# Eighteen differences and eighteen products of a chunked recurrence moved from GpSimd to VectorE, and two score copies from VectorE to ScalarE

## The reference, cut to what matters

```python
G = jnp.cumsum(gc, axis=2)
o_inter = jnp.einsum('bhtk,bhkv->bhtv', qc * jnp.exp(G), state)
diff = G[:, :, :, None, :] - G[:, :, None, :, :]
decay = jnp.exp(jnp.where(causal[:, :, None], diff, -jnp.inf))
scores = jnp.einsum('bhtsk,bhsk->bhts', qc[:, :, :, None, :] * decay, kc)
o_intra = jnp.einsum('bhts,bhsv->bhtv', scores, vc)
```

## Time and profile before

| | |
|---|---|
| median of 3 runs | 3371.41 us (3369.54 to 3372.2) |
| the profiled execution's own time | 3371.84 us |
| its span | 3370.0 us, so 1.84 us lie around it |
| PE busy over the span | 3061.2 us, 91% |
| DVE, ACT, POOL busy | 1454.9, 827.7, 849.2 us |
| the stage with the two mixers | about 430 to 767 us of the span |

### The profile page before, as it was taken

The page is one execution under the profiler, slowest core; times in us unless marked ns, Lnnn a source line. Parts: engine busy times, 40 slices in busy tenths (PEclk is TensorE's granted clock), DMA queues, the critical chain, the costliest instruction groups (busy, mean ns, idle before and its releaser), DMA issues.

```text
span 3370.0 us, 36149 instructions
## 1 busy us (share of the span) xinstructions
PE 3061.2 (91%) x15301; PEld 2521.8 (75%) x15301; DVE 1454.9 (43%) x2167; ACT 827.7 (25%) x1087; POOL 849.2 (25%) x555
## 2 busy tenths in 40 slices
PE   8889946569999999999999989799999999999997
PEld 7768735457788888887977889766667878787785
DVE  4766447754433333335325244311125443334335
ACT  3211232221211111221237222211111322222221
POOL 0332324441312111223311255300212111111113
PEclk9989966669999999999999999899999999999998
DMA  4112120112211111110311200211030111111111
GB/s 136 57 54 76 42 76 26 51 56 94 75 38 50 50 51 50 38 50 26 104 32 38 61 16 20 69 50 38 25 113 26 50 42 46 50 50 38 50 50 75
DMA packets 152513, 180.47 MB, mean 54 GB/s; under 512 B 6352, under 2 KB 127888, under 8 KB 152352
## 3 DMA queue, kind: packets, MB, share of 16 engines
q1 hardware_dynamic: 143680, 166.51, 15.9%
q10 hardware_dynamic: 8672, 11.65, 1.0%
HBM read 158.05 MB, written 20.09 MB: 53 GB/s over the span
## 4 chain that ended last, share of the span: by engine, by line
PE 76%; DVE 12%; POOL 4%; ACT 3%; issue 3%; DMA 2%; SPq 0%; ACTq 0%; DVEq 0%; POOLq 0%
PE bank L127 75%; DVE f L158 5%; POOL f L158 4%; DVE f L166 2%; PE bank L142 2%; DVE f L175 1%; ACT f L147 1%; DVE f L163 1%; DVE r L158 1%; DVE f L184 1%; ACT r L150 1%; DMA f<-gr_s 1%; ACT f L150 1%; DMA f<-x 0%; DMA f<-w_in 0%
## 5 line engine op out<-in xcount | busy, mean ns | idle before, releaser
L127 PE MATMUL bank<-r,r 128*128 128x512 f32 (+4 forms) x11592 | 2450.4, 372 | 48.3 <-DVE r L158 25.3
L127 PEld LDWEIGHTS bank<-r,r 128*128 128x128 f32 x11592 | 2018.9, 190 | 470.6 <-issue 52.1
L158 POOL TENSOR_TENSOR f<-f 128x512 f32<-128x512 f32 (+5 forms) x313 | 409.6, 1316 | 1770.6 <-ACT f L147 611.7
L158 DVE TENSOR_TENSOR f<-f,bank 128x512 f32<-128x512 f32 (+2 forms) x519 | 318.4, 635 | 453.4 <-PE bank L127 451.9
L127 PE MATMUL bank<-f 128*128 128x128 f32 (+7 forms) x2328 | 343.8, 317 | 115.8 <-DVE f L158 54.7
L158 DVE TENSOR_TENSOR r<-f,r 128x512 fp32r<-128x512 f32 (+3 forms) x169 | 227.6, 1354 | 511.2 <-ACT r L150 511.2
L127 PEld LDWEIGHTS bank<-f 128*128 128x128 f32 (+2 forms) x2328 | 295.7, 213 | 148.5 <-issue 76.4
L150 ACT ACTIVATE r<-f 128x2048 fp32r<-128x2048 f32 (+2 forms) x217 | 278.8, 1307 | 428.3 <-DMA f<-w_up 182.9
L166 DVE SCALAR_TENSOR_TENSOR f<-f,f 128x1024 f32<-128x1024 f32 (+2 forms) x153 | 196.4, 1288 | 347.5 <-ACT f L147 319.3
L158 POOL TENSOR_TENSOR r<-f,r 128x2048 fp32r<-128x2048 f32 (+1 forms) x48 | 219.8, 4579 | 443.4 <-ACT r L150 443.4
L147 ACT ACTIVATE f<-bank 128x512 f32<-128x512 f32 (+1 forms) x187 | 96.6, 518 | 939.4 <-PE bank L127 935.6
(11 more groups left out here) (31 smaller groups left out, 571.4 us busy)
## 6 DMA issues: line engine op xcount, KB each, us to landing
f<-w_in SPq DMA_DIRECT2D x31, 1024.0 KB, 6.1
f<-w_up SPq DMA_DIRECT2D x44, 512.0 KB, 5.1
f<-w_mlp_in SPq DMA_DIRECT2D x16, 1024.0 KB, 5.6
f<-w_mlp_out SPq DMA_DIRECT2D x16, 1024.0 KB, 4.9
f<-w_down SPq DMA_DIRECT2D x11, 1024.0 KB, 5.0
f<-w_out SPq DMA_DIRECT2D x8, 1024.0 KB, 5.3
f<-x_spill SPq DMA_DIRECT2D x4, 2048.0 KB, 11.8
f<-x SPq DMA_DIRECT2D x4, 1024.0 KB, 11.6
```

The source lines that it names most:

```text
L127: return self.g.matmul(out, lhs, rhs, start=start, stop=stop, skip_group_check=True)
L158: return self.g.tensor_tensor(out, a, b, op)
```

## The change

What it does, part by part:

- Levels 1 to 6: one VectorE instruction forms `G - pivot` over all 1024 columns ("level diff") in place of one half on VectorE and one on GpSimd. ScalarE takes two exponentials of 512 columns: of the high half, and of the low half with scale -1. VectorE makes `kt` behind the two `qt`. GpSimd has no level work left.
- Level 7 (n = 1): the high difference is the log decay `F` itself and the low one is zero. So no difference is formed, ScalarE reads the high columns of `F`, and TensorE takes `KK` itself in place of `KT`.
- The scores of levels 1 and 2 are copied by ScalarE without a mask, in blocks of partitions and columns: one instruction of 64 partitions for each half `h` at level 1, two of 32 partitions at level 2. VectorE's picks begin with level 3.
- ScalarE's copies stand in its program behind the exponentials of the level two further on, and ahead of the SSD work of that step.

```diff
@@ pe_hgrn
+                    Kt = S.KT[l % 2] if l < 7 else KK[:, NM:]
@@ act_hgrn
-                D = S.DD[(s + 1) % 2][:, 0:1024]
-                g.wait_ge(*k.past("diff low", i, s + 1))
-                g.wait_ge(*k.past("diff high", i, s + 1))
-                g.act(D, D, ACT.Exp).then_inc(*k.up("hgrn acts", "level exp", i, s + 1))
+                (dv, fv), lo, hi = level_parts(s + 1, S.DD[(s + 1) % 2][:, 0:1024], F[:, NM:])
+                if s + 1 < 7:
+                    g.wait_ge(*k.past("level diff", i, s + 1))
+                else:
+                    level_room(k, g, i, 7)
+                g.act(dv[:, :, hi], (dv if s + 1 < 7 else fv)[:, :, hi], ACT.Exp).then_inc(
+                    *k.up("hgrn acts", "level exp", i, s + 1))
+                if s + 1 < 7:
+                    g.act(dv[:, :, lo], dv[:, :, lo], ACT.Exp, scale=-1.0).then_inc(
+                        *k.up("hgrn acts", "level exp low", i, s + 1))
+            if s in (2, 3):
+                l, n = s - 1, LEVELS[s - 2]
+                for h in range(2):
+                    g.wait_ge(*k.past("score", i, l, h))
+                    g.wait_ge(*k.past("drain", "score", i, 0, h))
+                    b4 = k.bank("score", i, l, h).rearrange("p (c n b) -> p c n b", c=8, b=n)
+                    for x in range(64 // n):
+                        ss = slice(2 * n * x, 2 * n * x + n)
+                        o = SM[ss, 4 * h:4 * h + 4].rearrange("p c h t -> p (c h) t")[:, :, 2 * n * x + n:2 * n * x + 2 * n]
+                        ins = g.cp(o, b4[ss, :, x])
@@ dve_hgrn
-                g.tt(dv[:, :, hi], gv[:, :, hi], gv[:, :, n - 1:n].to_broadcast([128, 512 // n, n]), SUB).then_inc(
-                    *k.up("hgrn vec", "diff high", i, s + 1))
+                g.tt(dv, gv, gv[:, :, n - 1:n].to_broadcast([128, 512 // n, 2 * n]), SUB).then_inc(
+                    *k.up("hgrn vec", "level diff", i, s + 1))
+                if s < 7:
+                    (dv, kv, tv), lo, hi = level_parts(s, S.DD[s % 2][:, 0:1024], KK[:, NM:], S.KT[s % 2])
+                    g.wait_ge(*k.past("level exp low", i, s))
+                    g.tt(tv[:, :, lo], kv[:, :, lo], dv[:, :, lo], MUL).then_inc(*k.up("hgrn vec", "kt", i, s))
-            if s > 1:
+            if s > 3:
@@ pool_hgrn
-            if is_level(s + 1):
-                g.tt(dv[:, :, lo], gv[:, :, n - 1:n].to_broadcast([128, 512 // n, n]), gv[:, :, lo], SUB).then_inc(
-                    *k.up("hgrn pool", "diff low", i, s + 1))
-            if is_level(s):
-                g.wait_ge(*k.past("level exp", i, s))
-                factors_room(k, g, i, s)
-                g.tt(tv[:, :, lo], kv[:, :, lo], dv[:, :, lo], MUL).then_inc(*k.up("hgrn pool", "kt", i, s))
```

More of the change, by code:

```diff
@@ L1239, in one @@
                     cc = 4 * h + c
-                    ins = g.mm(b[:, 128 * c:128 * c + 128], S.KT[l % 2][:, 128 * cc:128 * cc + 128],
+                    Kt = S.KT[l % 2] if l < 7 else KK[:, NM:]
+                    ins = g.mm(b[:, 128 * c:128 * c + 128], Kt[:, 128 * cc:128 * cc + 128],
                                S.QT[l % 2][:, cc].rearrange("p h t -> p (h t)"))
@@ L1318, in one @@
             if is_level(s + 1):
-                D = S.DD[(s + 1) % 2][:, 0:1024]
-                g.wait_ge(*k.past("diff low", i, s + 1))
-                g.wait_ge(*k.past("diff high", i, s + 1))
-                g.act(D, D, ACT.Exp).then_inc(*k.up("hgrn acts", "level exp", i, s + 1))
+                (dv, fv), lo, hi = level_parts(s + 1, S.DD[(s + 1) % 2][:, 0:1024], F[:, NM:])
[18 more added lines that the diff above has]
+                        ins = g.cp(o, b4[ss, :, x])
+                        if x == 64 // n - 1:
+                            ins.then_inc(*k.drain("hgrn acts", "score", i, l, h))
             if i == 2 and s == 8:
@@ L1379, in one @@
         for s in range(9):
-            if is_level(s + 1):
+            if is_level(s + 1) and s + 1 < 7:
                 (gv, dv), lo, hi = level_parts(s + 1, GR, S.DD[(s + 1) % 2][:, 0:1024])
@@ L1396, in one @@
                 k.also("qt", i, s)
+                if s < 7:
+                    (dv, kv, tv), lo, hi = level_parts(s, S.DD[s % 2][:, 0:1024], KK[:, NM:], S.KT[s % 2])
+                    g.wait_ge(*k.past("level exp low", i, s))
+                    g.tt(tv[:, :, lo], kv[:, :, lo], dv[:, :, lo], MUL).then_inc(*k.up("hgrn vec", "kt", i, s))
+                else:
+                    k.also("kt", i, s)
             if s == 1:
@@ L1469, in one @@
         for s in range(9):
[L1470 to L1473, removed]
-                g.tt(dv[:, :, lo], gv[:, :, n - 1:n].to_broadcast([128, 512 // n, n]), gv[:, :, lo], SUB).then_inc(
-                    *k.up("hgrn pool", "diff low", i, s + 1))
-            if is_level(s):
-                (dv, kv, tv), lo, hi = level_parts(s, S.DD[s % 2][:, 0:1024], KK[:, NM:], S.KT[s % 2])
-                g.wait_ge(*k.past("level exp", i, s))
-                factors_room(k, g, i, s)
-                g.tt(tv[:, :, lo], kv[:, :, lo], dv[:, :, lo], MUL).then_inc(*k.up("hgrn pool", "kt", i, s))
             if s == 8:
```

## The result

The changed kernel takes 3358.49 us in the median of 7 runs (3351.59 to 3361.63), beside 3369.54 (3366.37 to 3372.37, 7 runs) of the kernel before on the same chip: ratio 0.9965, 95% interval 0.9953 to 0.9976. It is faster, by 11 us, where 12.3 had been forecast.

A forecast was written before the change was run, and what follows sets the result against it. No engine fills the two-mixer stage; a chain over DVE, POOL, ACT and PE's output products bounds it. Terms 0 - 5.1 - 2.2 + 0.4 - 4.0 - 0.2 - 1.2 = -12.3 us take 3371.4 to 3359 us; 8-in-10 range 3342 to 3371.

The forecast's parts named there:

- The bound: Stage of the two mixers, 430 to 767 us: no engine fills it, a chain of waits sets its length.
- Pair 0: Pair 0 alone, 481 to 560 us: level steps come out level with before, 0 with +-2 us.
- First output block: 583 to 604 us: `squares` no longer behind pair 1's level 1 picks, level 2 picks gone; -5.1 us.
- Pair 1's last levels: 604 to 650 us: difference gone, picks and SSD `diff` less slowed by GpSimd's level work; -2.2 us.
- Pair 2's start: 658 to 672 us: wider difference and `kt` added, low exponential ahead of the SSD squares; +0.4 us.
- Second block: Second output block, 674 to 701 us: `y rs0` 2.8 us earlier, then difference and picks against `kt`; together -4.0 us.
- To the end: -0.2 us at 704 to 711 us, -1.2 us from three less-slowed `diff`; tail from 733 us untouched.
- rival of a larger gain: Denser stage granted PE's upper clock at output blocks: -10 to -15 us more, so 3347 us; chance 0.18.
- Prices: Without GpSimd beside: 512-column exponential 0.62 us, 1024-column difference 1.23, a pair's copies 2 x 0.59 + 4 x 0.37 = 2.7.
- The ledger: DVE's net +11.4 us against up to 20 us of slowing lost: its work hardly changes, the question is where.
- No measurable change: Rival: DVE's extra 11.4 us lie on the path and the slowing stays; 3368 us, chance 0.19.
- Slower by ScalarE: Rival: strided exponentials cost nearly as much as whole ones, +19 us over 18 levels; 3378 us, chance 0.11.

The follow-up runs named there:

- the second measurement: The changed kernel timed and profiled once more, unaltered, on another group's chip: 3353.46 us, ratio 0.9948.
- Run 3: Kernel before, with only VectorE's two level 1 picks moved to the start of its step 3: 3358.58 us, ratio 0.9960.
- run 1: Kernel before, with level 1 and 2 scores copied by ScalarE and VectorE's picks from level 3; GpSimd keeps its level work: 3361.05 us, ratio 0.9962.
- run 6: Kernel before, with ScalarE score copies and the level 7 edit; GpSimd keeps differences and `kt` of levels 1 to 6: 3354.66 us, ratio 0.9944.
- run 8: Changed kernel, with every ScalarE score copy made twice, first into a spare tile: 3357.04 us, ratio 0.9953.
- run 7: Changed kernel without score copies, VectorE taking the level 1 picks at the start of its step 3: 3361.97 us, ratio 0.9968.
- run 2: Changed kernel without ScalarE's score copies; VectorE picks levels 1 and 2 again at their old place: 3365.82 us, ratio 0.9980.
- run 4: Changed kernel, with 42 unused GpSimd products of 128x512 where the old level work stood: 3370.09 us, ratio 0.9993.
- run 11: Kernel before, with the level 7 edit alone: 3370.44 us, ratio 0.9995.
- run 10: Changed kernel, with `kt` of levels 1 to 6 back on GpSimd, differences staying on VectorE: 3350.21 us, ratio 0.9943.

## Why the prediction was right, step by step

**The bound.** A chain through VectorE, with TensorE's output blocks in it: right. What was won at the marker stayed won: a long piece of products of the following stage, which starts at 885.18 us before, starts at 870.19, 15.0 us earlier. That the medians differ by 11 us where 12.3 had been forecast is closer than the measurement can bear: the interval reaches from 8 to 16 us, and the second measurement gave 17. The stage is where the forecast can be judged, -14.45 against -12.3, and step by step:

**Pair 0, 0 +-2.** Measured -1.0, inside, but as a sum of parts that I had not seen. By the levels column the copies bring -2.8, the level 7 edit with them another -1.1, and the move +2.9. I called the first two levels "a little late"; each was late by 1.26 us on VectorE, and what made it good was the two levels' missing picks. Behind the levels TensorE's clock at the outputs decides as much as all this: it made the two profiles of the changed kernel differ by 2.3 us there.

**First output block, -5.1.** Measured 591.08 to 585.85 for `squares`, -5.2 less the -1.0 brought along, and 599.83 to 593.06 at the SSD sum, -6.8: -5.7. What I put at 3.9 us behind `squares` takes 3.86 (589.28 to 593.14). Run 3 shows the cause apart from everything else.

**Pair 1's last levels, -2.2.** Measured -1.35, from 650.96 to 642.84 in the chain for the first output products. The mechanism (slowing gone) is there, `qt` at 784 ns, but I took it as a net gain where `kt` and the wide difference eat it. From the start of pair 1's level 3 scores (599.43 us before, 593.25 in the changed kernel) to these output products runs 1 and 6 take 49.6 us with the slowing still there, just as the changed kernel does, where the kernel before takes 51.5.

**Pair 2's start, +0.4.** +0.1, from 677.21 to 669.21.

**Second block, -4.0.** `y rs0` 692.33 to 681.35, -11.0, with -8.0 brought along: -3.0 (forecast -2.8), and another -1.2 behind it (forecast -1.2). What the copies' place ahead of `y squares` costs by itself is not shown: run 8, which doubles them, lost at most the 0.6 us there that its faster TensorE clock may have hidden.

**To the end, -1.4.** Measured -2.25. The term that was mis-sized is the piece of 48 products that starts at 733.54 before and at 720.10 after: 10.76 and 9.74 us. It ran at a granted clock of 0.50 before, the lower level of 1.2 GHz throughout, and of 0.56 after; its first four products took 1.63 and 0.92 us. The second profile of the changed kernel has 9.72 us. So 1.0 us of the 14.45 is TensorE's clock in this piece, and neither moved work nor order. I had put that into the rival of a larger gain, at the output blocks; there the 10.25 us piece takes 10.26 after, unchanged.

**Prices.** 0.62 for an exponential of 512 columns: 0.59. The budget of the Trainium skill (ScalarE: Activation LUTs, Rules for kernel authors), which the page gives for an instruction with its bias as a pointer operand, makes it an estimated 0.72. That is a fifth too high here, and the rows were right to be kept. Copies 2 x 0.59 + 4 x 0.37: exact. The difference of 1024 columns 1.23: 1.294. GpSimd in the stage 79: 82.2. 64x512 at 800 ns or below: 784. Idle time moved from VectorE's picks to waits for ScalarE at the output blocks, as said.

**The ledger.** "DVE's work hardly changes" was right (+1.4 us busy, with 14 us of the next stage in the window), and so was the view that what counts is where it changes. What the prediction didn't do is say what the move of levels 1 to 6 is worth by itself. It is a loss: 2.9 us in pair 0's levels, 2.7 to 4.8 at the marker counted from the entry, so by the profiles the change would be faster without it (run 6); whole runs don't separate the two. I had the price (+11.4 us of work against up to 20 of slowing) but not that the slowing is absent at pair 0's start, where the extra work has nothing to set against it.

**Rivals.** No measurable change: falls, by the interval. Slower by ScalarE: falls with 0.59 us, and run 8 shows ScalarE's slack. The larger gain: the clock gave 1.0 us at the piece ahead of the marker and not 10 to 15.

**What stays open.** Why `kt` and the differences cost less together than apart (2.9 us in pair 0's levels, against 2.3 and 1.8); and what decides when TensorE's clock falls. Ahead of the marker it falls about a microsecond later in both profiles of the changed kernel and in runs 7 and 8; at the second block runs 2, 3, 4 and 11 have 2 to 3 us less in TensorE's pieces than the kernel before, runs 6, 7 and 10 0.6; and at pair 0's outputs two profiles of the same kernel differ.

## What to carry to other kernels

On an engine that works in order, look first for a short instruction that waits for a busy engine while other chains' work stands behind it: moving two picks one step later, nothing else, gave as much as the whole change in the median, and 10.2 of its 14.45 us at the marker. Work taken from GpSimd to VectorE is paid by the slowing that it ends only where the two truly ran side by side; read each stretch for that, not the mean over the stage. And where whole runs differ by more than the effect, compare the start of one late instruction, but count it from one that lies ahead of everything that was changed, and lay the long pieces of TensorE side by side. Two profiles of one kernel had the late instruction within 0.2 us of each other when their spans differed by 10, and were still 2.1 us apart from the entry on; a stretch without long TensorE pieces on its path repeated within 0.1.

## What the runs showed of the hardware

- GpSimd's products cost VectorE far more than GpSimd's MEMSETs: 42 products of 1.49 us raised `qt` from 784 to 997 ns and lost 15.8 us at the marker, 84 MEMSETs of 0.526 us left it at 733 ns and lost 2.0. The MEMSETs did slow VectorE's TENSOR_SCALAR of 128x128, from 421 to 546 ns.
- A ScalarE copy from PSUM costs by columns: 64x512 594 ns as 128x512 at 593, 32x256 372 ns as 128x256 at 377. Two copies of 32 partitions are dearer than one of 64.
- A ScalarE exponential whose columns lie in strided halves costs no more than columns say: 0.59 us for 512, 1.056 for 1024.
- VectorE's `copy_predicated` of 128x512 has a mean of 943 ns over all seven levels and 1017 over levels 3 to 7. In pair 2 of the kernel before, two of them take 1.30 to 1.34 us together at levels 2 to 5 (blocks of 32 to 4 columns) and 2.46 and 2.44 at levels 6 and 7 (blocks of 2 and 1), so only the narrowest blocks are dear, and moving levels 1 and 2 moved cheap ones (VectorE's timeline, levels 5 and 6):

```profile
720.70 1.30 DVE L184 COPY_PREDICATED f<-f,bank 128x512 f32<-128x512 uint32 x2
...
726.85 2.46 DVE L184 COPY_PREDICATED f<-f,bank 128x512 f32<-128x512 uint32 x2
```

- TensorE's granted clock changes the same 32 products of one kernel between two profiles: 5.42 us at 0.66 and 6.74 at 0.50.
